# A decoder layer's expert down projection: 64 of 256 tokens from gathered rows of v, summed on VectorE

## The reference

```
q = (x_tok @ w_q).reshape(t, 8, 2, 128)
s = einsum('thpc,hpnc->thpn', q, sub_keys)
s1, i1 = top_k(s[:, :, 0], 16);  s2, i2 = top_k(s[:, :, 1], 16)
top_s, ci = top_k(all 16 x 16 sums, 16)
experts = e1 * 128 + e2;  g = softmax(top_s)
act = gelu(einsum('td,thkd->thk', x_tok, peer_u[experts]))
out = einsum('thk,thkd->td', act * g, peer_v[experts])
x = layer_norm(alpha * x1 + out)
```

## Time and profile before

| what | before |
|---|---|
| median of three runs | 1923.2 us |
| the profiled execution, its own time | 1925.2 us |
| its span in the trace | 1923.4 us |
| TensorE (PE) busy | 98% |
| VectorE (DVE), ScalarE (ACT), GpSimd (POOL) busy | 66%, 44%, 11% |
| mean traffic | 188 GB/s |

### The profile page before, as it was taken

The page is one execution under the profiler, slowest core; times in us unless marked ns, Lnnn a source line. Parts: engine busy times, 40 slices in busy tenths (PEclk is TensorE's granted clock), DMA queues, the critical chain, the costliest instruction groups (busy, mean ns, idle before and its releaser), DMA issues.

```text
span 1923.4 us, 34079 instructions
## 1 busy us (share of the span) xinstructions
PE 1888.8 (98%) x12650; PEld 1722.1 (90%) x12650; DVE 1276.0 (66%) x1847; ACT 854.6 (44%) x1080; POOL 221.1 (11%) x97
## 2 busy tenths in 40 slices
PE   8999999999999999999999999999999999999997
PEld 8999977899999999999999999888888888888776
DVE  7999975699847677777777755444444544444456
ACT  5544454344444444444444444444444444444442
POOL 0000024678940000000000000000000000000000
PEclk9999999999999999999999999999999999999999
DMA  7665546555565555555555556655655556555553
GB/s 272 222 209 187 196 155 221 187 175 174 167 201 179 178 178 179 175 178 179 178 176 179 178 182 201 213 190 187 232 189 188 177 193 188 189 188 188 187 176 130
DMA packets 98089, 361.78 MB, mean 188 GB/s; under 512 B 10848, under 2 KB 10976, under 8 KB 96480
## 3 DMA queue, kind: packets, MB, share of 16 engines
q1 hardware_dynamic: 97728, 360.49, 56.4%
q10 hardware_dynamic: 288, 0.44, 0.1%
HBM read 356.69 MB, written 4.19 MB: 188 GB/s over the span
## 4 chain that ended last, share of the span: by engine, by line
PE 95%; DVE 2%; issue 1%; POOL 1%; ACT 1%; DMA 0%; POOLq 0%; DVEq 0%; SPq 0%; ACTq 0%
PE psum L1184 18%; PE psum L1185 18%; PE psum L1186 17%; PE psum L1350 12%; PE psum L1351 12%; PE psum L1352 12%; PE psum L1318 2%; PE psum L1228 1%; PE psum L1230 1%; PE psum L1229 1%; POOL w_lo L437 1%; PE psum L1268 0%; DMA xt_raw<-in_x_t_dram 0%; DVE cacc L831 0%; DVE psum L745 0%
## 5 line engine op out<-in xcount | busy, mean ns | idle before, releaser
L468 ACT ACTIVATE w_hi<-raw 128x1024 fp32r<-128x1024 f32 x652 | 691.3, 1061 | 961.8 <-PE psum L1186 494.2
L665 DVE TENSOR_TENSOR w_lo<-raw,w_hi 128x1024 fp32r<-128x1024 f32 x568 | 693.8, 1227 | 481.6 <-ACT w_hi L468 480.0
L1184 PE MATMUL psum<-xt_hi,w_hi 128*128 128x256 f32 x2944 | 829.9, 282 | 15.9 <-DVE xt_lo L679 9.3
L1185 PE MATMUL psum<-xt_lo,w_hi 128*128 128x256 f32 x2944 | 824.1, 280 | 0.0
L1186 PE MATMUL psum<-xt_hi,w_lo 128*128 128x256 f32 x2944 | 822.6, 279 | 0.0
L1184 PEld LDWEIGHTS psum<-xt_hi,w_hi 128*128 128x128 f32 x2944 | 555.3, 189 | 18.0 <-issue 11.9
L1185 PEld LDWEIGHTS psum<-xt_lo,w_hi 128*128 128x128 f32 x2944 | 555.4, 189 | 0.0
L1186 PEld LDWEIGHTS psum<-xt_hi,w_lo 128*128 128x128 f32 x2944 | 555.2, 189 | 0.0
L1350 PE MATMUL psum<-w_hi,c_hi 128*128 128x512 f32 x1008 | 399.0, 396 | 1.8 <-DVE c_lo L1085 1.8
L1352 PE MATMUL psum<-w_hi,c_lo 128*128 128x512 f32 x1008 | 398.7, 396 | 0.0
L1351 PE MATMUL psum<-w_lo,c_hi 128*128 128x512 f32 x1008 | 398.7, 396 | 0.0
(11 more groups left out here) (147 smaller groups left out, 861.9 us busy)
## 6 DMA issues: line engine op xcount, KB each, us to landing
raw<-in_u_w_dram SPq DMA_DIRECT2D x256, 512.0 KB, 3.3
raw<-in_v_w_dram SPq DMA_DIRECT2D x256, 512.0 KB, 3.9
raw<-in_w_in_dram SPq DMA_DIRECT2D x80, 512.0 KB, 3.4
raw<-in_w_out_dram SPq DMA_DIRECT2D x32, 512.0 KB, 3.3
raw<-in_w_q_dram SPq DMA_DIRECT2D x32, 512.0 KB, 3.3
xt_raw<-in_x_t_dram SPq DMA_DIRECT2D x4, 512.0 KB, 8.4
acc<-in_x_nat_dram SPq DMA_DIRECT2D x1, 2048.0 KB, 7.9
x_spill<-acc SPq DMA_DIRECT2D x1, 2048.0 KB, 6.4
```

The lines of the kernel that those rows point to most:

```text
L468: nc.scalar.activation(parts_of(slot_u)[0][:, :], raw[:, slot_u % RAW, :], ACT.Copy).then_inc(hi_done, 1)
L665: tt(lo_w[:, :], raw[:, slot_u % RAW, :], hi_w[:, :].bitcast(f32), ALU.subtract).then_inc(lo_done[slot_u % SPLIT], SPLIT)
L1184: mm(dst, hi_w[:, sl], xt_hi[:, kk, :], start=st, stop=False)
L1185: mm(dst, hi_w[:, sl], xt_lo[:, kk, :], start=False, stop=False)
```

## The change

The last 64 tokens (SPARSE) leave the dense down projection; 192 (TD) stay.

- **Dense part.** The gate matrix has 192 tokens, 24 batches. For block 0 all stays. For block 1 a coefficient operand `both` of 128 columns holds the high part of tokens 128 to 191 in its first 64 columns and their low part in the other 64. Two matmuls (with w_hi and w_lo) replace three. The two halves of the resulting 128 rows still have to be added.
- **Sparse part.** In the up projection ScalarE writes the gelu of the last 64 tokens to a ring `stage` in SBUF and stores it, four tiles at a time, to DRAM (`acts_out`, 32 stores). After the routing, ScalarE loads the 64 tokens' selections into sp_sel: partition p has token p % 64 and half of the heads, so 64 picks a partition. VectorE works out row numbers (`selections`, at tile 24).
- **Gathers.** GpSimd issues indirect transfers, each of 128 rows by an index column: for each pick k the activation (`gather_acts`, 4 bytes a row, 64 in all, in bursts of 16), and four chunks of the row of v, 2 KB a row (`gather_rows`, 256 in all), into a ring of four row buffers. Two picks are gathered before the store of the activations is complete.
- **Sum.** VectorE multiplies activations by gates (`pick_coefs`) and adds each row times its coefficient to `picked` (128 x 2048), at units U_DOWN + 14 + 208 k // 64, in the order loop of the low parts.
- **Fold.** For each chunk, ScalarE and VectorE split block 1's bank and the chunk of `picked` into high and low parts, and four matmuls with a constant matrix `fold` add the halves and put the 64 dense and 64 sparse tokens into their rows. Folds 0 and 1 stand in the third chunk, 2 and 3 in the last.
- **Order of the end.** In the last chunk block 1 comes first, then block 0; the tail does block 1, then block 0. Three chunks go over ScalarE and GpSimd instead of one.
- **Queues.** The residual's reload moves from SP's place before the third round of v (after unit 8) to behind unit 64, waiting for the coefficients of group 5; the norm's parameters move behind unit 96. GpSimd makes `fold` (iota, memset, add, copy) between its low parts of w_q and of u.

The core of the diff:

```
-NB = T // BATCH
+SPARSE = 64
+TD = T - SPARSE
+NB = TD // BATCH
+HALVES = P // SPARSE
+PICKS = HEADS * TOPK // HALVES
+ROWS = 4
+PICKS_IN = 16
+PART_OF_TILE = 6
+STAGE = 12
+STORED = 4
...
+FOLD_AT = {2: 0, 6: 1}
+LN2_VECTOR = [(1, 0), (1, 1), (0, 0), (0, 1), (0, 2)]
+LN2_POOL = [(1, 2), (1, 3), (0, 3)]
+def pick_unit(k):
+    return U_DOWN + 14 + (U_LAST - U_DOWN - 16) * k // PICKS
...
+        split_at = {U_LAST + 2 * LAST * (j + 1) + 3: j for j in range(NCH - 2)}
+        split_at[U_LAST + 2 * LAST * (NCH - 1) + 5] = NCH - 2
...
+            def gather_rows(k):
+                if k >= ROWS:
+                    pool.wait_ge(picked_done, k - ROWS + 1)
+                elif k >= 2:
+                    pool.wait_ge(used, USED0 + U_DOWN)
+                for j in range(NCH):
+                    nc.gpsimd.indirect_dma_start(
+                        rows[k % ROWS][:, j * DCH:(j + 1) * DCH], None, v_rows,
+                        bass.IndirectOffsetOnAxis(sp_idx[:, 1 + j, k:k + 1], 0)).then_inc(rows_in[k % ROWS], 16)
+            def gather_acts(n):
+                for k in range(PICKS_IN * n, PICKS_IN * (n + 1)):
+                    nc.gpsimd.indirect_dma_start(
+                        sp_act[:, k:k + 1], None, act_dram,
+                        bass.IndirectOffsetOnAxis(sp_idx[:, 0, k:k + 1], 0)).then_inc(act_in[n], 16)
+            pool.wait_ge(idx_done, 1)
+            pool.wait_ge(sel_tr, 1)
+            for k in range(2):
+                gather_rows(k)
+            pool.wait_ge(stage_out, 16 * (N_KEYS // STORED))
+            gather_acts(0)
+            for k in range(2, ROWS):
+                gather_rows(k)
+            for n in range(1, PICKS // PICKS_IN):
+                gather_acts(n)
+                for k in range(ROWS + 8 * (n - 1), ROWS + 8 * n):
+                    gather_rows(k)
+            for k in range(ROWS + 8 * (PICKS // PICKS_IN - 1), PICKS):
+                gather_rows(k)
...
+            def acts_out(c):
+                c0 = c - STORED + 1
+                act.wait_ge(gelu_done, PART_OF_TILE * (c + 1))
+                if c0:
+                    act.wait_ge(stage_out, 16 * (c0 // STORED))
+                act.dma_start(act_tiles[:, c0:c0 + STORED, :], stage[:, c0 % STAGE:c0 % STAGE + STORED, :])\
+                    .then_inc(stage_out, 16)
...
+            def pick(k):
+                if k % PICKS_IN == 0:
+                    pick_coefs(k // PICKS_IN)
+                dve.wait_ge(coef_done, k // PICKS_IN + 1)
+                dve.wait_ge(rows_in[k % ROWS], 16 * NCH * (k // ROWS + 1))
+                if k == 0:
+                    i = ts(picked[:, :], rows[0][:, :], sp_coef[:, 0:1], None, ALU.mult)
+                else:
+                    dve.wait_ge(picked_done, k)
+                    i = stt(picked[:, :], rows[k % ROWS][:, :], sp_coef[:, k:k + 1], picked[:, :], ALU.mult, ALU.add)
+                i.then_inc(picked_done, 1)
...
+                    if 0 in blocks:
+                        mm(v_bank(j, 0), hi_c[:, n, :], w1, start=st, stop=False)
+                        mm(v_bank(j, 0), hi_c[:, n, :], w2, start=False, stop=False)
+                        i = mm(v_bank(j, 0), lo_c[:, n, :], w1, start=False, stop=en)
+                    if 1 in blocks:
+                        mm(v_bank(j, 1), both_c[:, n, :], w1, start=st, stop=False)
+                        i = mm(v_bank(j, 1), both_c[:, n, :], w2, start=False, stop=en)
...
+            def fold_chunk(j):
+                pe.wait_ge(split_lo, 2 * j + 2)
+                dense, sparse = fold[:, SPARSE:3 * SPARSE], fold[:, 0:2 * SPARSE]
+                mm(v_bank(j, 1), dense, y_part[j % 2][0][:, :], start=True, stop=False)
+                mm(v_bank(j, 1), dense, y_part[j % 2][1][:, :], start=False, stop=False)
+                mm(v_bank(j, 1), sparse, s_part[j % 2][0][:, :], start=False, stop=False)
+                mm(v_bank(j, 1), sparse, s_part[j % 2][1][:, :], start=False, stop=True).then_inc(folded, 1)
...
+            for b in (1, 0):
                 for g in range(G_LAST, GROUPS):
                     for h in range(2):
                         u = down_unit(g, NCH - 1) + h
+                        i = down(u, u, NCH - 1, h, c_sets[coef_slot(g)], [b], False, g == GROUPS - 1)
+                        if not b:
                             i.then_inc(used, 1)
+                            if (g, h) == (G_LAST + 1, 1):
+                                fold_chunk(2)
+                            if (g, h) == (G_LAST + 3, 0):
+                                fold_chunk(3)
```

More of the change, by code:

```diff
@@ L133, in build, with coefs @@
         oh1 = sb("oh1", [P, OUTER, N_KEYS, INNER], bf16)
+        def coefs(name, where):
+            return [sb(f"{name}_{part}", [P, GROUP, P], f32r, where) for part in ("hi", "lo", "both")]
         down0 = ExitStack()
-        c_pairs = [[sb("c_hi0", [P, GROUP, T], f32r, down0), sb("c_lo0", [P, GROUP, T], f32r, down0)]]
+        c_sets = [coefs("c0", down0)]
         down0.close()
@@ L219, in parts_of @@
             return w_hi[u % SPLIT], w_lo[u % SPLIT]
-        hid = sb("hid", [P, N_KEYS, T], f32)
+        hid = sb("hid", [P, N_KEYS, TD], f32)
+        folds = ExitStack()
+        y_part = [[sb(f"y{i}_{part}", [P, DCH], f32r, folds) for part in ("hi", "lo")] for i in range(2)]
+        s_part = [[sb(f"s{i}_{part}", [P, DCH], f32r, folds) for part in ("hi", "lo")] for i in range(2)]
+        folds.close()
+        rows = [sb(f"rows{i}", [P, D], f32) for i in range(2)] + rows_late
+        stage = sb("stage", [P, STAGE, SPARSE], f32)
+        picked = sb("picked", [P, D], f32)
+        sp_sel = sb("sp_sel", [P, 3, PICKS], f32)
+        sp_u = sb("sp_u", [P, 3, PICKS], u32)
+        sp_f = sb("sp_f", [P, 3, PICKS], f32)
+        sp_row = sb("sp_row", [P, 1 + NCH, PICKS], f32)
+        sp_idx = sb("sp_idx", [P, 1 + NCH, PICKS], u32)
+        sp_act = sb("sp_act", [P, PICKS], f32)
+        sp_coef = sb("sp_coef", [P, PICKS], f32)
+        sp_tok = sb("sp_tok", [P, 2], f32)
+        fold_f = sp_row[:, 0:3, :].rearrange("p a k -> p (a k)")
+        fold = sb("fold", [P, 3 * SPARSE], f32r)
         x1_dram = nc.dram_tensor("x1_spill", [TB, P, D], f32, kind="Internal").ap()
+        act_dram = nc.dram_tensor("act_spill", [N_KEYS * N_KEYS * SPARSE, 1], f32, kind="Internal").ap()
+        act_tiles = act_dram.rearrange("(c p t) o -> p c (t o)", c=N_KEYS, p=P, t=SPARSE)
+        v_rows = v_w.rearrange("u p (e c) -> (u p e) c", c=DCH)
         psum = ctx.enter_context(nc.psum_tensor("psum", [P, 8, DCH], f32))
@@ L571, in gelu @@
                 act.wait_ge(used, USED0 + U_UP + 2 * c + 2)
-                parts = [(hid[:, c, n:T], n, T)] if n < T else []
+                if c == 0:
+                    act.wait_ge(x1_out, 16)
+                if c >= STAGE and c % STORED == 0:
+                    act.wait_ge(stage_out, 16 * ((c - STAGE) // STORED + 1))
+                parts = [(stage[:, c % STAGE, :], TD, T)]
+                if n < TD:
+                    parts.append((hid[:, c, n:TD], n, TD))
                 if n:
@@ L1108, in _ @@
                     gates_in(m - 1)
+                if c == GATE0 + 4:
+                    selections()
                 if c == COEF0_AT:
@@ L1362, in group @@
                     if first and j == 3:
[L1363 removed]
+                        pe.wait_ge(gelu_done, PART_OF_TILE * N_KEYS)
                     for h in range(2):
                         n = 2 * j + h
[L1366 removed]
+                        down(U_DOWN + 2 * NCH * g + n, U_DOWN + n, j, h, c_sets[slot], [0, 1], first)\
                             .then_inc(used, 1)
```

234 lines of the change are left out of this document (164 added, 70 removed).

## The result

The kernel after takes 1905.7 us (median of 13 runs, 1898.2 to 1919.3), against 1923.3 for the kernel before on the same chip (13 runs). The ratio is 0.9908, 95% interval 0.9890 to 0.9925. So it is 0.9% faster, where 1811 us (5.8%) was forecast; it lies 11 us above the range. The profiled execution took 1898.2 us around a span of 1896.4, at the lower end of the runs.

The account below looks back on a forecast made before the run. TensorE's matmul count times pace was taken as the bound: 1925.2 - 126.8 (matmuls, gates) + 3.7 (folds) + 3.0 (collisions) + 2.7 (gathers) + 2.0 (up start) + 3.6 (tail) = 1813.4, against the median 1811 us; range 1802 to 1895.

Parts of the forecast that it names:

- VectorE fits: Down stage: VectorE's work per eight units takes 16.5 us of 18.7, bringing it from 48% to 88% busy.
- The 3 us of collisions: Down stage: allowance for row additions delaying VectorE's low parts; 0 if none, 28 us if each is missed.
- the worst place: Group's first unit with a row addition behind the coefficients: low part ready at 9.0 us, TensorE wants it at 9.3.
- I take 1.27 us: Down stage: assumed GpSimd time per gather issue, from its 512-element instruction's row; costs 2.7 us in the sum.
- 6 + 44c + 3: Down stage: when gathered row 4 is there, in us from stage start; wanted at 63.
- c: GpSimd's time in us to issue one gather in the down stage; bounds 0.39 and 2.4 to 2.6.
- 20c - 25: Down stage: no stall while 20c, a 16-gather burst plus four issues, stays under the 25 us four row buffers allow.
- 312c + 9: Down stage: us GpSimd needs if its rate alone sets the stage, against 509 planned; for c above about 1.95.
- rival 1: Down stage: GpSimd issues gathers slower than assumed; 1857 us at c = 1.6, 1932 at 2.0; chance 0.23.
- Rival 2: Down stage: GpSimd's gathers and VectorE's two-operand work shut each other out; 2079 us at d = c = 1.27; chance 0.12.
- d: Us each gather holds VectorE off in the down stage; decides above 0.22, the gain is gone at 0.65.
- Rival 3: Down stage: v lands too late; five-unit lap L + 6.0 us, landing L = 6.2: 25 us more, 1836; chance 0.13.

Follow-up runs that it names:

- Experiment 1: Kernel after without GpSimd's gathers and the row sums (`picked` set to zero once): 1808.0 us, ratio 0.9395 to the kernel before.
- experiment 11: Kernel after without activation gathers and with row gathers of 512 B in place of 2 KB, sums at full length: 1808.5 us.
- experiment 2: Kernel after without the 64 activation gathers (coefficients made of other numbers), row gathers and sums kept: 1836.4 us.
- experiment 5: Kernel after with memory for GpSimd's pending gathers doubled (1024 to 2048) and 8 stage buffers in place of 12: 1881.1 us.
- experiment 6: Kernel after with one 8 KB gather per row in place of four of 2 KB, and doubled memory for pending gathers: 1859.0 us.
- 10: Kernel after with one 8 KB gather per row, later activation gathers spread behind rows, doubled pending-gather memory, 12 stage buffers: 1838.6 us.

## Why the prediction was wrong

**Right: what was removed, and the ends.** Experiment 1 stands 2.7 us above 1811 - 3.0 - 2.7 = 1805.3, and the kernel before was 0.7 us above the forecast's base beside it. The down projection started 8.0 us earlier; the gate batches were to give 7.4, and the 2 us put on GpSimd's operations at the start of the up stage didn't come. The tail grew by 3.8 us (forecast 3.6), with the last addition 3.3 us behind TensorE as worked out.

**Right: VectorE fits.** The additions took 2.36 us (2.28 taken), the coefficients' two pieces 0.69 + 0.42 = 1.11 (1.1 taken), and experiment 11 has the 88% nearly to the letter. The 3 us of collisions are 0.5 there. So the worst place, where the sum of waits came to within 0.3 us of TensorE's, never cost anything that can be measured.

**The step that failed: "I take 1.27 us" for one gather issue.** The lone issue is that long, 0.94 us and a gap of 0.30, though that is luck: the row came from arithmetic of GpSimd. But it was priced as an instruction by itself. Beside VectorE's two-operand work it stretches to 2 us and more, and after seven gathers of a burst GpSimd stands until older ones are out of the way; with both it is 1.85 us. The formulas around it held. Row 4, after 44 issues, was to be there at 6 + 44c + 3 into the stage; with the 1.82 us of those 44 issues (1190.3 to 1270.2) that is 89, and it was 87.1. It was wanted at 63, and VectorE asked at 66. At c = 1.85 a row of four issues takes 7.4 us of its 7.58, so the eight rows between two bursts regain only 1.4 us (20c - 25 holds while the buffers are full again by the next burst), and by the prediction's way of counting a later burst loses 16c - 1.4 = 28 us. VectorE waited 19.2 and 26.1 us there. In all that is 27 + 2 x 28 = 84 us late, and 1811 - 3 + 84 = 1892; by the rate alone, 312c + 9 = 586 us for the 509 planned, it is 77 late and 1885. Of the 14 to 21 us that are missing to 1905.7, part is likely the half clock after each stall and part v's late landings; the runs don't split them.

So rival 1 was the case (chance 0.23), priced there at c = 1.6, and at 1.85 its price would have come within 14 us. The bounds 0.39 and 2.6 did hold c. The mistake was to take one row by its likeness to a gather, when the gathers were to run beside a VectorE busy for 88%, and to set 2.7 us for a term that nothing in the trace priced.

**Rival 2 had the clash right and the direction wrong.** By the traces GpSimd's issues lengthen and VectorE's instructions don't (1224 ns against 1227), so d is 0, not 1.27. What the prediction held against this rival, that tensor_tensor was not seen to stall a transfer issued by GpSimd, is not so for these gathers: the issue at 1276.58 took 1.98 us beside low parts, which are TENSOR_TENSOR. The Trainium skill (SBUF — State Buffer, Who interferes with whom) says that the side that comes first blocks the other. The trace agrees for GpSimd's side: an issue caught by an addition of 2.35 us took up to 3.08 in place of 0.94. It doesn't for VectorE's: with 312 issues beside them, no group of its instructions in the down stage is longer.

**Rival 3 was real, beside the main cause.** It priced v's late landing at 25 us, 1836 in all. Once the activation gathers are out of the way that is what remains: 28.4 us, 1836.4. That the size fits so well is partly luck: it took a landing of 6.2 us, and with the median of 5.7 that experiment 2 shows, its own lap gives (5.7 + 6.0) / 5 = 2.34 us a unit, next to nothing.

**What was missing from the list** is a limit on gathers under way. No row of before could show it. Lifting it brings 24.6 us as the kernel stands, and 165 us with the spread order, which by any count of issues should have been the better.

## What to carry to other kernels

Price a GpSimd gather by its rate in company, not by its instruction: here 1.25 us alone, 1.7 beside a VectorE with two-operand work and 1.85 with the pauses, nearly whatever it fetches (1.68 is 346.4 us busy and 71.3 of gaps for 248 row gathers in experiment 5). So make few large ones (one of 8 KB instead of four of 2 KB gave 37 us), and no long burst ahead of one that somebody waits for (spreading it gave 20 us from experiment 6 to 10). When GpSimd stands for some us with nothing named in the trace after the same count of gathers each time, enlarge the memory of its pending gathers before changing the order of work.

## What the runs showed of the hardware that was not expected

- In a burst of activation gathers, with 1024 bytes for pending gathers GpSimd pauses after 7 gathers of 128 pieces, with 2048 after 14. The pauses are 2 to 4.7 us. The count is no period of all gathers: in the kernel after, 17 gathers went out without a pause from 1219.47 to 1247.93, eight of them of rows.
- A gather of 128 single numbers isn't cheap: seven of them and the pause took 14.3 us (1190.31 to 1204.60), 2.0 us each, though they move 3.5 KB in all. Over the stage the kernel after spent 1.86 us of GpSimd on each of them, and 1.85 on each row gather of 256 KB.
- VectorE's two-operand instructions lengthen a gather's issue from 0.94 us to 2 or 3; the gather doesn't lengthen them (1221 ns with gathers, 1225 without).
- After TensorE had stood still for some us, the granted clock read 0.50 (1.2 GHz) and was still 0.53 in the window in which it resumed.
